# Forget-gate attention over two slots per head, with gate and modulation matmuls between its steps, and output projections by halves

## What is computed

```
mod = silu(c) @ w_ada + b_ada                      # 6 x 1024: sh1, sc1, g1, sh2, sc2, g2
h   = x * (1 + sc1) + sh1
rq, rk, rv, rg, fq, fk, fv, ff, ga, gb = split(h @ w_in + b_in)
y_ret = (silu(rg) * GroupNorm_heads(Retention(rot(rq), rot(rk), rv))) @ w_ret_proj      # 4 heads
y_fox = ForgettingAttention(fq, fk, fv, log_sigmoid(ff)) @ w_fox_proj                   # 16 heads of 64
x   = LN1(alpha * x + (1 + g1) * ((sigmoid(ga) * y_ret + sigmoid(gb) * y_fox) @ w_o))
h   = x * (1 + sc2) + sh2
x   = LN2(alpha * x + (1 + g2) * HierMoE(h))       # top 1 of 4 groups, then top 2 of its 8 experts
```

## Time and profile before

| what | value |
| --- | --- |
| median of 3 runs | 1290.4 us (1285.68 to 1293.38) |
| the profiled execution's own time | 1293.22 us |
| its span | 1291.4 us |
| TensorE (PE) busy | 1093.0 us, 85% |
| VectorE (DVE) busy | 926.1 us, 72% |
| ScalarE (ACT) busy | 683.7 us, 53% |
| GpSimd (POOL) busy | 202.7 us, 16% |
| granted TensorE clock, mean of the span | 0.868 |
| memory traffic | 303.67 MB, 235 GB/s |

### The profile page before, as it was taken

How to read it: one execution, slowest core, us unless ns; L and a number is a source line. 1 busy time by engine, 2 the same in 40 slices (tenths; PEclk the granted TensorE clock), 3 DMA queues, 4 the chain that set the end, 5 groups by cost and what they waited for, 6 DMA issues and landing times.

```text
span 1291.4 us, 12580 instructions
## 1 busy us (share of the span) xinstructions
PE 1093.0 (85%) x4643; PEld 802.2 (62%) x4643; DVE 926.1 (72%) x997; ACT 683.7 (53%) x677; POOL 202.7 (16%) x171
## 2 busy tenths in 40 slices
PE   5989989799999999998646988888889888889960
PEld 2657757487775666686545656666667666666640
DVE  6848763484643333464966899999998999998957
ACT  5542550331313222333023867888887888887942
POOL 0006601110011000002604032111111101011000
PEclk9899999899995555798856997999998999999985
DMA  9947877182761000337117998999999999999923
GB/s 331 319 125 236 234 209 205 58 231 87 172 195 41 0 0 0 114 130 244 38 41 255 346 344 307 355 378 382 385 379 381 358 385 397 381 388 365 380 112 117
DMA packets 85710, 303.67 MB, mean 235 GB/s; under 512 B 10148, under 2 KB 10196, under 8 KB 68758
## 3 DMA queue, kind: packets, MB, share of 16 engines
q1 hardware_dynamic: 74200, 278.56, 61.5%
q0 software_dynamic: 9152, 20.19, 4.7%
q10 hardware_dynamic: 2304, 4.20, 1.1%
HBM read 299.71 MB, written 14.73 MB: 243 GB/s over the span
## 4 chain that ended last, share of the span: by engine, by line
PE 47%; DVE 35%; issue 8%; ACT 7%; DMA 2%; SPq 0%; ACTq 0%; POOLq 0%; DVEq 0%
DVE w_lo L1621 22%; PE banks L1783 9%; PE banks L1777 9%; PE banks L1779 6%; PE banks L2060 4%; ACT w_hi L968 4%; DVE w_lo L1091 3%; PE banks L2055 2%; PE banks L1810 1%; PE banks L2047 1%; ACT w_hi L793 1%; PE banks L2067 1%; PE banks L1944 1%; PE banks L1935 1%; DVE y_pair L1648 1%
## 5 line engine op out<-in xcount | busy, mean ns | idle before, releaser
L1621 DVE TENSOR_TENSOR w_lo<-w_raw,w_hi 128x2048 fp32r<-128x2048 f32 x192 | 441.9, 2328 | 29.0 <-ACT w_hi L968 28.1
L968 ACT ACTIVATE w_hi<-w_raw 128x2048 fp32r<-128x2048 f32 x192 | 361.5, 1905 | 18.1 <-PE banks L2060 18.1
L1091 DVE TENSOR_TENSOR w_lo<-w_raw,w_hi 128x2048 fp32r<-128x2048 f32 x68 | 163.0, 2414 | 83.8 <-ACT w_hi L793 83.8
L793 ACT ACTIVATE w_hi<-w_raw 128x2048 fp32r<-128x2048 f32 x68 | 128.7, 1911 | 162.0 <-PE banks L1783 147.9
L2060 PE MATMUL banks<-w_lo,xT_pair 128*128 128x512 f32 x512 | 155.7, 428 | 33.2 <-DVE w_lo L1621 32.1
L2055 PE MATMUL banks<-w_hi,xT_pair 128*128 128x512 f32 x512 | 151.1, 419 | 23.5 <-ACT w_hi L968 20.0
L2060 PEld LDWEIGHTS banks<-w_lo,xT_pair 128*128 128x128 f32 x512 | 95.0, 199 | 83.5 <-DVE w_lo L1621 66.3
L1777 PE MATMUL banks<-w_hi,h_hi 128*128 128x512 f32 x384 | 142.5, 412 | 4.5 <-ACT w_hi L793 4.5
L2055 PEld LDWEIGHTS banks<-w_hi,xT_pair 128*128 128x128 f32 x512 | 98.0, 199 | 50.1 <-DVE xT_pair L1627 25.9
L1783 PE MATMUL banks<-w_lo,h_hi 128*128 128x512 f32 x384 | 109.4, 408 | 8.6 <-DVE w_lo L1091 8.6
L736 POOL DMA_INDIRECT scratch_y<-y_pair,slot_row x16 | 35.6, 2224 | 478.6 <-DVE y_pair L1648 420.4
(11 more groups left out here) (440 smaller groups left out, 1452.6 us busy)
## 6 DMA issues: line engine op xcount, KB each, us to landing
w_raw<-in_w_e_in SPq DMA_DIRECT2D x128, 1024.0 KB, 6.5
w_raw<-in_w_e_out SPq DMA_DIRECT2D x64, 1024.0 KB, 7.2
w_raw<-in_w_in SPq DMA_DIRECT2D x32, 1024.0 KB, 9.4
w_raw<-in_w_ada SPq DMA_DIRECT2D x24, 1024.0 KB, 9.2
bias_rows<-in_b_in ACTq DMA_DIRECT2D x16, 256.0 KB, 5.8
w_raw<-in_w_ret_proj SPq DMA_DIRECT2D x4, 1024.0 KB, 8.2
w_raw<-in_w_fox_proj SPq DMA_DIRECT2D x4, 1024.0 KB, 6.6
w_raw<-in_w_o SPq DMA_DIRECT2D x4, 1024.0 KB, 5.0
```

The costliest lines, as they stand in the source:

```text
L793: nc.scalar.activation(whi[n % NSPL][:], raw[n % NRAW][:], ACT.Copy).then_inc(hi_done, 1)
L968: nc.scalar.activation(whi[n % NSPL][:], raw[n % NRAW][:], ACT.Copy).then_inc(hi_done, 1)
L1091: V.tensor_tensor(wlo[n % NSPL][:], raw[n % NRAW][:], whi[n % NSPL][:].bitcast(F32), ALU.subtract).then_inc(lo_done, 1)
L1621: V.tensor_tensor(wlo[n % NSPL][:], raw[n % NRAW][:], whi[n % NSPL][:].bitcast(F32), ALU.subtract).then_inc(lo_done, 1)
```

## The change

**The order of chunks.** `CH` now has rk, rv0, rv1, rg0, rg1, ga0 and ga1 without ada chunks between them. ada4 to ada11, gb0 and gb1 come behind fv1, and the eight halves of pf and wo alternate.

**Slots.** The hardware loops of the attention are unrolled. Slot h holds `head_T(h+1)`, the parts that a table `BETWEEN` gives it, `weighted(h-1)`, `scores(h+1)` and `probs_T(h)`. A part is a third of a dense half (t0, t1 or t2) or half an ada chunk. Slots 0 to 3 and 6 to 9 hold gb0 and gb1, slots 4, 5 and 10 an ada chunk each, slots 11 to 16 half of one; ada4 stands ahead of the slots and ada11 behind them. The staging copies go: TensorE reads the q, k and v rows where they lie, and the scale of q moves to `copy_q`. ACT copies all transposed probabilities in one operation and writes out each head without normalising; DVE normalises eight heads at a time (`normalised`).

**Banks.** All dense and ada chunks use banks 0 to 2 up to pf0, the attention and the other transposes 3 to 7. On DVE the new `advance` evacuates a chunk between the two `lo` of the next one.

**Retention.** The heads' scores and values alternate with the six parts of ga1; fk1 stands behind the transposes of the retention output. Rotary products, the decay table and the retention state come earlier on POOL.

**Output projections.** The halves come as pf0.0, pf1.0, pf0.1, pf1.1, wo0.0, wo1.0, wo0.1, wo1.1, with the transposes of four blocks at a time between them.

**Buffers.** The ring `w_raw` has four buffers up to the MoE and six in it; the other two lie where the attention's tiles, the parts of c, the modulation rows and the residual lie before, and are first filled when all chunks are evacuated. POOL waits for the end of the attention, not of pf1, before it loads the residual again.

```diff
-    NRAW, NSPL = 6, 3
+    NPRE, NRAW, NSPL = 4, 6, 3
...
-    CH = ["ada0", "ada1", "ada2", "ada3", "rq", "ada4", "rk", "ada5", "rv0", "ada6", "rv1", "ada7", "rg0", "ada8",
-          "ada9", "rg1", "ada10", "ada11", "ga0", "ga1", "fq0", "fq1", "fk0", "fk1", "pr0", "pr1", "fv0", "fv1",
-          "gb0", "gb1", "pf0", "pf1", "wo0", "wo1"]
+    CH = ["ada0", "ada1", "ada2", "ada3", "rq", "rk", "rv0", "rv1", "rg0", "rg1", "ga0", "ga1", "fq0", "fq1", "fk0", "fk1",
+          "pr0", "pr1", "fv0", "fv1", "ada4", "gb0", "ada5", "ada6", "gb1", "ada7", "ada8", "ada9", "ada10", "ada11",
+          "pf0", "pf1", "wo0", "wo1"]
+    HALVES = [(n, s) for n in CH[:-4] for s in range(2)]
+    HALVES += [("pf0", 0), ("pf1", 0), ("pf0", 1), ("pf1", 1), ("wo0", 0), ("wo1", 0), ("wo0", 1), ("wo1", 1)]
...
+    BETWEEN = {0: [("gb0", 0, 0)], 1: [("gb0", 0, 1), ("gb0", 0, 2)], 2: [("gb0", 1, 0)], 3: [("gb0", 1, 1), ("gb0", 1, 2)],
+               4: [("ada5", 0, 0), ("ada5", 1, 0)], 5: [("ada6", 0, 0), ("ada6", 1, 0)], 6: [("gb1", 0, 0)],
+               7: [("gb1", 0, 1), ("gb1", 0, 2)], 8: [("gb1", 1, 0)], 9: [("gb1", 1, 1), ("gb1", 1, 2)],
+               10: [("ada7", 0, 0), ("ada7", 1, 0)], 11: [("ada8", 0, 0)], 12: [("ada8", 1, 0)], 13: [("ada9", 0, 0)],
+               14: [("ada9", 1, 0)], 15: [("ada10", 0, 0)], 16: [("ada10", 1, 0)]}
...
-    def dense_banks(w):
-        return (0, 1, 2) if w % 2 == 0 else (3, 4, 5)
...
+    def plan_dense(n, banks=(0, 1, 2)):
...
+        def advance(upcoming, drain, name):
+
+            lo(TILE[(upcoming, 0)])
+            drain(name)
+            lo(TILE[(upcoming, 1)])
...
-        for h in range(RH):
+        pe.wait_ge(qkT_done, 2 * RH)
+        ret_scores(0)
+        part("ga1", 0, 0, actH, actL)
...
+        for h, (s, t) in enumerate(((0, 1), (0, 2), (1, 0))):
+            ret_values(h)
+            ret_scores(h + 1)
+            part("ga1", s, t, actH, actL)
+        ret_values(RH - 1)
+        part("ga1", 1, 1, actH, actL)
+        part("ga1", 1, 2, actH, actL)
...
-        with pe.Fori(1, FH - 1) as h:
+        for h in range(FH):
+            if h + 1 < FH:
+                head_T(h + 1)
+            between(h)
+            if h == 0:
+                pe.wait_ge(evacuated, CI["fv1"] + 1)
+            else:
+                weighted(h - 1)
+            if h + 1 < FH:
+                scores(h + 1)
             probs_T(h)
+        between(FH)
+        weighted(FH - 1)
+        ada(11)
...
+        pe.wait_ge(fox_norm, 1)
+        blocks_T("fox", fox_rows, range(4))
+        pe.wait_ge(fox_norm, 2)
+        half("pf0", 0, foxH, foxL, split_ready("fox"))
+        blocks_T("fox", fox_rows, range(4, KD))
+        half("pf1", 0, foxH, foxL)
+        half("pf0", 1, foxH, foxL, split_ready("fox"))
+        part("pf1", 1, 0, foxH, foxL)
+        part("pf1", 1, 1, foxH, foxL)
+        pe.wait_ge(evacuated, CI["pf0"] + 1)
+        blocks_T("mix", mix_rows, range(4))
+        part("pf1", 1, 2, foxH, foxL)
+        half("wo0", 0, mixH, mixL, split_ready("mix"))
         pe.wait_ge(evacuated, CI["pf1"] + 1)
+        blocks_T("mix", mix_rows, range(4, KD))
+        half("wo1", 0, mixH, mixL)
+        half("wo0", 1, mixH, mixL, split_ready("mix"))
+        half("wo1", 1, mixH, mixL)
```

More of the change, by code:

```diff
@@ L427, in build_layer @@
         plan_dense(n)
     fox_start = dict(free_at)
-    for b in range(8):
+    for n in CH[CH.index("ada4"):CH.index("pf0")]:
+        plan_dense(n)
+    for b in spare:
         free_at[b] = (o_ok, FH)
-    for k in range(KD):
-        plan(("fox", k), k)
-    for n in ("gb0", "gb1", "pf0", "pf1"):
-        plan_dense(n)
-    for k in range(KD):
-        plan(("mix", k), spare("pf1")[k % 5])
-    for n in ("wo0", "wo1"):
-        plan_dense(n)
+    for k in range(4):
+        plan(("fox", k), 3 + k)
@@ L439, in build_layer @@
+    plan_dense("pf0")
+    for k in range(4, KD):
+        plan(("fox", k), 6 + k % 2)
+    plan_dense("pf1", (3, 4, 5))
+    for k in range(4):
+        plan(("mix", k), 6 + k % 2)
+    plan_dense("wo0")
+    for k in range(4, KD):
+        plan(("mix", k), 6 + k % 2)
+    plan_dense("wo1", (3, 4, 5))
     for t in range(3):
@@ L949, in _ @@
+        hi(TILE[("pf1", 1)])
+        hi(TILE[("wo0", 0)])
+        split_hi("mix", mixH, range(4))
+        hi(TILE[("wo1", 0)])
+        split_hi("mix", mixH, range(4, KD))
+        hi(TILE[("wo0", 1)])
+        hi(TILE[("wo1", 1)])
         act.wait_ge(ln_var, 1)
@@ L1215, in _ @@
         for j in range(1, 4):
-            chunk(f"ada{j}")
+            for s in range(2):
+                lo(TILE[(f"ada{j}", s)])
             if j == 1:
@@ new lines, in part, with half, dense @@
+            if t == 0:
+                pe.wait_ge(lo_done, n + 1)
+            for kk in range(4):
+                last = mm(b[:, :], H[:, 4 * s + kk, cols], wlo[n % NSPL][:, kk, :], start=False, stop=(s == 1 and kk == 3))
+            if t == 2:
+                last.then_inc(used, 1)
+            elif s == 1:
+                last.then_inc(use[(name, t)][2][0], 1)
+        def half(name, s, H, L, ready=None):
+            for t in range(3):
+                part(name, s, t, H, L, ready)
+        def dense(name, H, L, ready=None):
+            half(name, 0, H, L, ready)
+            half(name, 1, H, L, ready)
```

662 lines of the change are left out of this document (296 added, 366 removed).

## The result

The changed kernel took 1226.0 us (median of 4 runs, 1223.23 to 1229.7), the kernel before 1291.21 beside it (4 runs, 1285.68 to 1293.38). The ratio is 0.9486, with an interval of 0.9453 to 0.9519. The forecast was 1227. The two profiled spans are 1291.4 and 1227.7, so the difference to be explained is 63.7 us, and the mean granted clock rose from 0.868 to 0.916. The profile after is of the execution that took 1229.7 us, the slowest of the four.

What follows compares the result with a forecast made beforehand. TensorE was taken to set the time of the dense stage, attention and what follows. -27.2 - 17.7 - 24.8 + 6 = -63.7 from 1293.2 gives 1229.5, as a median 1227; range 1199 to 1262, its own 1212 to 1244.

Steps and rivals of the forecast that it cites:

- The dense stage: Up to the qk transposes: six ada chunks leave, the zf wait goes and a hole shrinks; -27.2 us.
- The zf wait: Dense stage: the zf matmuls' 1.79 us wait for `wf_lo` goes, as DVE computes it ahead of evacuating rq; -1.8 us.
- the hole: Dense stage, behind rk up to the end of rv0: 10.7 us lost shrink to 7.7; -3.0 us.
- The seams costed at nothing: Other seams between dense chunks, sharing one set of banks: no cost expected; up to 3.1 us each if uncovered.
- Retention and what follows: Retention up to the attention: ada10 and ada11 leave, head waits and stalls shrink; -17.7 us, ends -14.8 and -30.3.
- The three waits left: Retention stage: stalls of 2.8 us before fq0, about 3 before fq1 and 1.8 before the transposes remain.
- Attention and projections: Attention and output projections: 246 us before become 221.2, including 11 us for falls of the clock; -24.8 us.
- the steps at full clock: Attention: a head's period of 8.28 us at half clock, 4.14 at full clock, is taken as 4.6.
- The end: `evac_wo` beside POOL's modulation operations ends 11 us behind TensorE; +6 us, ends 0 and +9.
- Rival 1: Clock stays at 1.2 GHz in the attention's steps: 1286 us, 1338 if dense parts run at half clock too; chance 0.16.
- Rival 2: Stalls are hidden and the clock holds throughout: 1200 us; chance 0.14.
- Rival 3: ACT or DVE becomes the bound of an attention slot, 2 us a slot: +32, 1259 us; chance 0.10.

Runs made afterwards that it cites:

- e1: Changed kernel with hi of rv0's first half ahead of the cfT copy, and hi of fq0's first half ahead of the merge gate's sigmoid: 1214.96 us.
- e2: Changed kernel with POOL's eight modulation operations on 8 of 1024 columns; measured up to the router, as its total of 1463.49 says nothing on the change.
- e4: Changed kernel with pf0, pf1, wo0 and wo1 as whole chunks, transposes of eight blocks ahead of pf0 and wo0: 1222.26 us.
- e3: Changed kernel with no dense or ada parts in the slots; gb0, gb1 and ada5 to ada10 stand behind the last head: 1295.29 us.
- e8: Changed kernel with the same dense and ada parts in every second slot only, ada10 behind the last head: 1258.85 us.
- e5: Changed kernel with both hi moved earlier, POOL's modulation operations after the attention, and four fox transposes between the halves of ada11: 1210.57 us.
- e12: Kernel with early hi, split ada11 and modulation rows loaded early, plus ada11 emptied before normalisation and POOL's modulation held until pf1 is evacuated: 1204.12 us.
- e7: Changed kernel with each of the 24 transposes of the retention output issued four times: 1226.68 us (one run).
- e9: Kernel without dense or ada parts in the slots, plus 16 unused identity transposes in each slot: 1257.94 us (one run).
- e11: Kernel without dense or ada parts in the slots, plus 8 unused identity transposes in each slot: 1263.2 us (one run).

## Why the prediction was right

**The dense stage: -28.9 for -27.2.** The zf wait and the six ada chunks went as priced. Of the hole, the wait was 5.17 for 5.0, and the half clock behind it 2.8 for the 2.7 put down (rv0 took 17.8 us in place of 14.97). The seams costed at nothing cost nothing: rv1, rg0 and rg1 run from 103.04 to 147.95, 14.97 each. The miss of 1.7 lies there all the same: before, the same three chunks and four ada chunks took 62.3 us (113.28 to 175.61) for 59.8 of work, and the 2.5 lost between them, which went too, were not in the sum.

**Retention and what follows: -21.3 for -17.7.** The three waits left came at 2.69, 1.49 and 1.46 for 2.8, 3 and 1.8, so the count of what ACT and DVE have ahead was good for two and pessimistic for fq1. One head waits 0.55, where 1.0 was left. The half clock was put at 5 and is 2.6, all of it behind the last wait: nine transposes took 2.75 us where 1.7 is the pace of those before them, and the next eight matmuls 3.44 where they take 1.87 at full clock. Behind the waits of 2.69 and 1.49 the matmuls ran at full clock at once. These small misses have one sign and add up to 4.8; about 1.2 the other way was not traced.

**Attention and projections: -21.5 for -24.8.** The decisive choice, the steps at full clock near 4.14 and not near 8.28, was right: 4.8 for the 4.6 taken. What failed are two smaller terms. The steps: +3. The waits: where one chain at the end was counted at 2.3, there are five, 6.1 us together. ada5 and ada7 wait 1.31 each for the evacuation of gb0 and gb1 from the banks that they share, slot 12 waits 1.25, ada10 and ada11 1.08 and 1.10 for lo. The clock fell behind two of them, to 0.60 over 380 to 384 and to 0.71 and 0.77 over the 13 us behind 453, which cost about the 5 us put down for the slots; a granted clock over 0.9 from the first slot to the last, the sign named, was so missed at two places. The values of heads 10 to 12 so begin at 444.73, 452.77 and 462.11, 8.0 and 9.3 us apart where the prediction had 6.5 for such slots. The seam where one chunk follows another inside a slot got no price, though the same seam was weighed for the dense stage. The wait in slot 12 comes from DVE's queue, where the normalisation of the first eight heads stands ahead of that slot's maxima:

```profile
448.27 1.89 DVE L1368 TENSOR_TENSOR fox_o<-fox_o,prob_inv 128x512 f32<-128x512 f32 x3
450.09 0.27 DVE L1356 TENSOR_REDUCE neg_max<-banks 128x1 f32<-128x128 f32 x1
```

Such waits are not always followed by a fall. In e1 the attention has the same ones, 1.31 at ada5 and ada7 and 1.23 in slot 12, and the clock behind each is 1.00; behind the last:

```profile
439.00:447.00 8.00, 7.14 (x44) 4.82 (x44) 5.06 (x7) 5.72 (x15) 0.00 (x0) 1.00 0.32 95
```

Together heads and their parts took 148.25 for 140.7. The projections took 76.7 for the 80.5 that 74.5 and the 6 of half clock give, so half of the miss came back: the wait for the merge is 0.55 for the 2.94 put down, the one at pf0 3.04 for 2.52. The half clock was 2.6 for the 6 put down: the 24 matmuls from 491.32 to 499.51 take 8.2 us where they take 5.6 at full clock. The price of some 3 us for a fall of the clock so held (2.8 behind rv0, 2.6 here and at the retention's transposes). But the rows 9 from which it was read were misread: the first matmul of gb0 there is at 528.11 and the pace changes at 533.3, so 5.2 us into dense work and not about 4.

**The end: +5.4 for +6**, by the mechanism named, which e2 shows: without POOL's load the end falls from 10.4 to 4.1. e4 adds what the prediction did not weigh: it is the halves of the projections that bring `evac_wo` and POOL's operations together, and on balance they gain nothing.

**What cancelled.** The sum met 63.7 to a tenth, while the runs of the changed kernel alone lie 6.5 us apart; the terms missed by 1.7, 3.6, 3.3, 0.6, 1.2 and 1.3. The forecast stands on its mechanism; the last digits are luck.

**The rivals.** Rival 1, the clock staying at 1.2 GHz, did not come, but its mechanism is real: e3 is that kernel, at 1295 for the 1286 named, and e8 lies halfway. Rival 2 (all stalls hidden) is what e1, e5 and e12 approach step by step; 1204 for its 1200. Rival 3 came in one slot only, the wait of 1.25 in slot 12, at a clock of 1.00 up to there; from 345 to 375 TensorE is busy 30.00 of 30.00 us, DVE 12.28, ACT 14.11.

**The rule weighed there.** The Trainium skill's page "TensorE: Matmul & The Clock Gate", Part 4, says that the full clock does not engage for transpose mode, which does not count as busy in the same way. For the float32 transposes of this kernel e7 and e9 speak against it: 11.4 us of transposes end at a granted clock of 1.00, and transposes alone, as filler, hold at 1.00 the heads that sit at 0.50 without them.

Still open: what makes e11's slots change from one kind to the other. The slots hold the same work, and the trace shows no cause. And whether it is the filled wait or the added work that holds the clock is not separated: every run that filled the waits also added work, and the same wait was followed by a lower clock in one kernel's trace and not in another's.
